# One channel group of a convolution moved to GpSimd, and the projection order of two blocks rewritten

## The chip, the cores and the metric

The kernel is written by hand for one NeuronCore of a Trainium2 chip, all in float32. The metric is the time of one execution on the device in microseconds (us), as the median of several runs. The engines are named as in the profile: PE (TensorE, matmuls), DVE (VectorE), ACT (ScalarE), POOL (GpSimd), SP (the queue that issues most transfers). Each runs its own instruction list in order; they meet only at semaphores.

## What is computed

Two stages of a transformer over 256 tokens of width 1024: two blocks of a first kind (the change touches only these), then two of a second kind. Cut to what matters, one block of the first kind is

```python
h = rms_norm(x, attn_norm_g[layer])
proj = einsum('bsd,de->bse', h, w_in[layer])
q, k_c, v_c, k_s, v_s, k_w, v_w, g_logit, u = split(proj)
q = rope_partial(rms_norm(q), positions)                  # 8 heads of 64
k_cmp, v_cmp = compress_blocks(k_c), compress_blocks(v_c) # 15 blocks of 32 tokens, a GELU MLP
k_cmp, k_slc, k_win = each rope_partial(rms_norm(k))      # 2 heads each
gates = sigmoid(g_logit)
attn_out = nsa_attention(q, k_cmp, v_cmp, k_slc, v_s, k_win, v_w, gates)
a, g = split(u, 2); y = conv(a * sigmoid(g), conv_w, 31 taps, per channel) + conv_b
conv_out = silu(layer_norm(y, ln_g, ln_b))                # 512 channels
x = x + concat(attn_out, conv_out) @ w_out[layer]
x = x + feed_forward(rms_norm(x))                         # dense in block 0, 8 experts in block 1
```

## The kernel before

The weights stream once from memory through a ring of six slots of 1 MB, in the order in which PE uses them. PE makes every product; most of the time of the kernel is PE streaming weight tiles.

The front of a block of the first kind is ordered by a table, `FRONT` (L48), which the programs of SP, PE, ACT and DVE all walk. An item is one weight tile or one small step: `u0` to `u3` (inputs of the convolution), `kv` (keys and values to be compressed), `q0`, `q1` (query heads, 4 each), `s0`, `s1` (the keys and values of two branches), `cmp0`, `cmp1` (the first products of the compression), `g` (gates), `ht`, `w2`, `gt` (small transposes and the second product of the compression), and `ada` (a tile of a matrix that only the second stage needs; 24 a block, of which 12 stand in the front to fill it).

Each item's product goes to one of two PSUM banks, `pt0` and `pt1`, strictly in turn: `bank()` (L807) counts items and takes bank n % 2, and PE waits until whoever read that bank two items earlier has emptied it. The reader is ACT for `ada` (`mod_rows`, L1577) and DVE for the others. ACT first squares the tiles of `q` and `s` (L1751, L1753) for the norm of the heads.

DVE's list, `taps(count)` (L2470), holds the convolution: a tap is one multiply-add of 128x256 for each of the 4 channel groups, all on DVE, `y` and `padded` both in SBUF:

```python
go(ve.scalar_tensor_tensor(out=y[:, cc, :], in0=src, scalar=wk, in1=y[:, cc, :],
                           op0=ALU.mult, op1=ALU.add))
```

`TAPS_AFTER` (L2538) says how many taps follow which item; 24 of the 31 stand in the front, the other 7 in `conv_beside` (L2602), 2 after each of the first attention batches. All 12 heads (8 of queries, 4 of keys) are normed and rotated together, after the last key tile and after `g`: `s1` brings one sum over the squares (L2559 to L2561) and ACT's square root, `g` the scaling (`head_scale`, L1892) and the rotation (`rotate`, L1896). Then PE transposes queries, keys and compressed keys (L1490 to L1506), DVE copies them, and the first scores can start (L894). POOL does almost nothing in this part.

## Time and profile before

| | us |
|---|---|
| median of 3 runs | 2905.27 |
| the three runs | 2900.3, 2905.27, 2907.2 |
| the profiled execution's own time | 2901.29 |
| its span, first to last instruction | 2899.5 |
| PE busy in it | 2730.1 |
| DVE busy in it | 1274.2 |
| ACT busy in it | 437.5 |
| POOL busy in it | 85.2 |

The table is read from the page of one profiled execution. Busy means that an instruction of the engine was running; an engine can be busy and yet not hold up the end. The front of the first block lies between about 30 and 146 us, that of the second between about 540 and 644 us; the attention that follows them takes some 80 us each.

### The profile page before, as it was taken

How to read it: one execution, taken by the hardware profiler on the slowest of the kernel's cores; microseconds unless marked ns; L12 is line 12 of the kernel's file. 1: busy time of each engine (PE TensorE's matmuls, PEld its weight loads, DVE VectorE, ACT ScalarE, POOL GpSimd, SP SyncE). 2: the span in 40 equal slices, each digit the busy share in tenths (PEclk: the TensorE clock that was granted, in tenths of full speed). 3: DMA queues.
4: the chain of work that ended last, by engine and by line, in shares of the span. 5: the costliest groups of instructions: out<-in, count | busy, mean ns of one | idle time of the engine just before them, and what ended most of it. 6: DMA issues, size and time to landing. Idle time of an engine off the chain costs nothing.

```text
span 2899.5 us, 49343 instructions
## 1 busy us (share of the span) xinstructions
PE 2730.1 (94%) x20757; PEld 1729.9 (60%) x20757; DVE 1274.2 (44%) x3076; ACT 437.5 (15%) x1031; POOL 85.2 (3%) x118
## 2 busy tenths in 40 slices
PE   7889999888899999999999998899989999988998
PEld 5657994665433333333333366679658967765993
DVE  1863666386301111111111155556665665233666
ACT  1131000124010110111101111400040001022100
POOL 1000000000000000000000010100000000032000
PEclk9969999988999999999999999999999999999999
DMA  8644555564499999999999955245514553122442
GB/s 260 204 146 146 164 172 174 176 203 146 168 347 397 381 409 388 385 411 387 401 398 385 403 192 105 49 145 162 174 58 145 162 174 122 67 73 61 158 167 96
DMA packets 311235, 634.95 MB, mean 219 GB/s; under 512 B 15161, under 2 KB 197825, under 8 KB 294512
## 3 DMA queue, kind: packets, MB, share of 16 engines
q1 hardware_dynamic: 305552, 616.09, 58.9%
q0 software_dynamic: 4800, 13.56, 2.6%
q8 instruction: 166, 2.72, 0.4%
q10 hardware_dynamic: 672, 2.21, 0.2%
q14 instruction: 45, 0.37, 0.0%
HBM read 623.98 MB, written 7.84 MB: 218 GB/s over the span
## 4 chain that ended last, share of the span: by engine, by line
PE 86%; DVE 9%; issue 2%; DMA 1%; POOL 1%; ACT 1%; PEld 0%; PEldq 0%; DVEq 0%; POOLq 0%; SPq 0%; ACTq 0%
PE pacc L1043 13%; PE pacc L1117 10%; PE pt L869 9%; PE pt L1117 7%; PE pt L1043 6%; PE pacc L1081 6%; PE pacc L1143 5%; PE pt L1143 5%; PE pacc L984 4%; PE po L1117 3%; PE pt L1081 3%; PE pt L1470 2%; PE pt L1022 2%; DVE bigc L2480 2%; PE pacc L894 1%
## 5 line engine op out<-in xcount | busy, mean ns | idle before, releaser
L2230 DVE TENSOR_TENSOR gateb<-kT,pt 128x512 f32<-128x512 f32 (+1 forms) x32 | 19.9, 621 | 477.6 <-PE pt L1117 476.9
L1117 PE MATMUL pacc<-ring,bigc 128*32 128x512 f32 (+1 forms) x1920 | 188.6, 550 | 4.5 <-issue 3.1
L869 PE MATMUL pt<-ring,hT 128*128 128x256 f32 x832 | 187.2, 384 | 3.6 <-issue 2.1
L869 PEld LDWEIGHTS pt<-ring,hT 128*128 128x128 f32 x832 | 157.3, 191 | 30.6 <-issue 9.3
L1043 PE MATMUL pacc<-probT,prob 128*128 128x128 f32 x1440 | 170.6, 275 | 0.0
L1043 PEld LDWEIGHTS pacc<-probT,prob 128*128 128x128 f32 x1440 | 165.6, 192 | 0.0
L1117 PEld LDWEIGHTS pacc<-ring,bigc 128*32 128x32 f32 x1920 | 68.4, 110 | 123.0 <-issue 121.0
L1117 PE MATMUL pt<-ring,bigc 128*32 128x512 f32 (+1 forms) x1280 | 139.5, 550 | 0.0
L1143 PE MATMUL pacc<-ring,bigc 128*32 128x512 f32 x864 | 137.9, 595 | 0.0
L1081 PE MATMUL pacc<-prob,chunks 128*128 128x512 f32 x282 | 136.4, 592 | 0.0
L2047 DVE TENSOR_TENSOR prob<-ring 128x512 f32<-128x512 f32 x86 | 59.5, 692 | 153.1 <-PE pacc L1043 106.4
L1143 PE MATMUL pt<-ring,bigc 128*32 128x512 f32 x1056 | 125.0, 592 | 0.0
L1625 ACT ACTIVATE prob<-prob,den 128x256 f32<-128x256 f32 (+3 forms) x192 | 99.2, 518 | 150.0 <-DVEq L1961 146.1
L984 PE MATMUL pacc<-ring,hT 128*128 128x512 f32 x256 | 111.3, 593 | 0.9 <-DVEq L2033 0.9
L842 PE MATMUL pt<-const,prob 128*128 128x128 f32 (+2 forms) x456 | 72.0, 300 | 37.0 <-DVEq L1821 33.0
L869 PE MATMUL pt<-ring,prob 128*128 128x256 f32 x448 | 103.8, 393 | 2.7 <-DVEq L2185 1.7
L2480 DVE SCALAR_TENSOR_TENSOR bigc<-big,convw,bigc 128x256 f32<-128x256 f32 x240 | 100.4, 481 | 4.4 <-DVE hid L2528 0.5
L869 PEld LDWEIGHTS pt<-ring,prob 128*128 128x128 f32 x448 | 87.9, 198 | 16.8 <-issue 3.1
L1698 ACT ACTIVATE kT<-pacc 128x512 f32<-128x512 f32 (+1 forms) x48 | 26.1, 544 | 471.2 <-PE pacc L1117 471.2
L1081 PEld LDWEIGHTS pacc<-prob,chunks 128*128 128x128 f32 x282 | 53.6, 190 | 67.4 <-issue 67.4
L1117 PEld LDWEIGHTS pt<-ring,bigc 128*32 128x32 f32 x1280 | 46.2, 110 | 77.4 <-issue 77.4
L1043 PE MATMUL pacc<-hT,ring 128*128 128x128 f32 x736 | 89.7, 275 | 0.0
(424 smaller groups left out, 4328.3 us busy)
## 6 DMA issues: line engine op xcount, KB each, us to landing
ring<-in_moe_w_down SPq DMA_DIRECT2D x80, 1024.0 KB, 13.8
ring<-in_w_gate_up SPq DMA_DIRECT2D x66, 1024.0 KB, 5.1
ring<-in_w_ada SPq DMA_DIRECT2D x48, 1024.0 KB, 5.5
ring<-in_moe_w_gate SPq DMA_DIRECT2D x48, 1024.0 KB, 6.1
ring<-in_moe_w_up SPq DMA_DIRECT2D x48, 1024.0 KB, 16.3
ring<-in_w_down SPq DMA_DIRECT2D x33, 1024.0 KB, 4.9
ring<-in_moe_w_gate SPq DMA_DIRECT2D x32, 768.0 KB, 11.4
ring<-in_moe_w_up SPq DMA_DIRECT2D x32, 768.0 KB, 8.4
```

The costliest lines, as they stand in the source:

```text
L842: return pe.transpose(dst, src, ident[0:n, 0:n])
L869: ins = pe.matmul(t[:, q * 256:q * 256 + n], src[:, k, q * P:q * P + P], w[:, k, 0:n], start=(k == 0), stop=(k == KC - 1))
L984: ins = pe.matmul(pacc[:, o:o + 512], src[:, kc, q * P:q * P + P], w[:, k, h * 512:h * 512 + 512], start=(kc == 0), stop=(kc == KC - 1))
L1022: ins = pe.matmul(pt[cc][:, j * S + lo:j * S + lo + P], tiles[j][:, k, cc * P:cc * P + P], half(k, q), start=(k == 0), stop=(k == KC - 1))
L1043: ins = pe.matmul(bank_[:, o:o + P], left(k), right(k), start=(k == 0), stop=(k == 3))
L1081: ins = pe.matmul(down_bank[m][:, 0:512], left[m], right[m], start=(g == 0), stop=(g == groups - 1), skip_group_check=True)
L1117: ins = pe.matmul(((X, Y, Z) if kind == "g" else up_bank)[r][32 * j:32 * j + 32, 0:w], hcurv[:, kc, 32 * g:32 * g + 32], moe_view(tile_)[: ...
L1143: ins = pe.matmul(banks[0 if j < 3 else i][32 * j:32 * j + 32, :], actT[:, f, 32 * g:32 * g + 32], w[:, f - 4 * t, :], start=(t == 0 and ( ...
L1470: ins = pe.matmul(t[:, h * S + lo:h * S + hi], w[:, k, h * P:h * P + P], hTv[:, k, lo:hi], start=(k == 0), stop=(k == KC - 1))
L1625: act.activation(prob[:, o:o + b.nk], prob[:, o:o + b.nk], ACT.Exp, scale=-1.0, bias=den[:, 8 + (i % 4) * 4 + j:9 + (i % 4) * 4 + j], accu ...
L2047: go(ve.tensor_tensor(s1, a21, a22, ALU.add))
L2480: go(ve.scalar_tensor_tensor(out=y[:, cc, :], in0=src, scalar=wk, in1=y[:, cc, :], op0=ALU.mult, op1=ALU.add))
```

## The change

It does four things in the two blocks of the first kind.

1. The order `FRONT`: an `ada` tile moves between `cmp0` and `s0`, and `g` moves from behind `w2` to a place ahead of `ht` and `s1`.
2. The 8 query heads are summed after `q1` and scaled and rotated after `s0`; the 4 key heads are summed after `s1` and scaled and rotated after `w2`. `qk_ready` is told twice. The square root is taken twice.
3. The fourth channel group of the convolution goes to POOL: for each tap a product into a free part of `ug` and a sum onto `y`, 31 taps a block, with semaphores. DVE's tap has three multiply-adds, and DVE waits for POOL's last tap after attention batch 3.
4. The number of taps after each item changes; their sum in the front stays 24.

```diff
-FRONT = ("ada ada cols u0 ada u1 ada u2 ada u3 ada kv ada ada q0 ada q1 ada cmp0 s0 cmp1 ada ht s1 w2 g ada gt".split(),
-         "u0 ada u1 ada u2 ada u3 ada kv ada ada q0 ada ada q1 ada cmp0 s0 ada cmp1 ada ht s1 w2 g ada gt".split())
+FRONT = ("ada ada cols u0 ada u1 ada u2 ada u3 ada kv ada ada q0 ada q1 ada cmp0 ada s0 cmp1 g ht s1 w2 ada gt".split(),
+         "u0 ada u1 ada u2 ada u3 ada kv ada ada q0 ada ada q1 ada cmp0 ada s0 cmp1 ada g ht s1 w2 ada gt".split())
...
+            for l in range(2):
+                pool.wait_ge(conv_padded, l + 1)
+                for k in range(TAPS):
+                    wk = convv[:, POOL_CHANNEL, l * TAPS + k:l * TAPS + k + 1]
+                    src = padded[:, POOL_CHANNEL, k:k + S]
+                    if k == 0:
+                        o = COL["conv_b"] + CC * l + POOL_CHANNEL
+                        pool.tensor_scalar(y[:, POOL_CHANNEL, :], src, wk, colA[:, o:o + 1], ALU.mult, ALU.add)\
+                            .then_inc(conv_tap, 1)
+                    else:
+                        pool.tensor_scalar(ug[:, k % 2, :], src, wk, None, ALU.mult).then_inc(conv_product, 1)
+                        pool.wait_ge(conv_product, l * (TAPS - 1) + k)
+                        pool.wait_ge(conv_tap, l * TAPS + k)
+                        pool.tensor_tensor(y[:, POOL_CHANNEL, :], y[:, POOL_CHANNEL, :], ug[:, k % 2, :], ALU.add)\
+                            .then_inc(conv_tap, 1)
...
+                pe.wait_ge(qk_ready, due("qk_ready"))
                 t, filled, uses, emptied = bank()
                 pe.wait_ge(emptied, uses)
                 for br in range(2):
...
-                        if item == "s1":
-                            root(small[:, 64:88])
+                        if item in ("q1", "s1"):
+                            root(head_sums[:, :, 0:8] if item == "q1" else head_sums[:, :, 8:12])
...
-                        for cc in range(CC):
+                        for cc in [c for c in range(CC) if c != POOL_CHANNEL]:
...
-                TAPS_AFTER = {"kv": 4, "q0": 5, "q1": 5, "cmp0": 3, "s0": 4, "ht": 3}
+                TAPS_AFTER = {"kv": 4, "q0": 5, "q1": 5, "cmp0": 4, "g": 1, "ht": 5}
+
+                def sum_heads(lo, hi):
+                    r = head_sums[:, :, lo:hi]
+                    link(ve.tensor_reduce(r, sqv[:, :, lo:hi, :], AX.X, ALU.add))
+                    link(ve.tensor_scalar(r, r, 1.0 / HD, EPS, ALU.mult, ALU.add))
+                    link(ve.reciprocal(r, r))
+                    tell(root_in)
+
+                def norm_heads(lo, hi):
+                    n = hi - lo
+                    ve.wait_ge(root_out, due("root_out"))
+                    heads = qkz[:, :, lo:hi, :]
+                    link(ve.tensor_tensor(heads, heads, free(head_sums[:, 0:1, lo:lo + 1], [[12, QT], [1, n], [0, HD]]),
+                                          ALU.mult))
+                    for q in range(QT):
+                        rotate(...)
+                    ve.sem_inc(qk_ready, 1)
...
                         link(ve.tensor_tensor(padded[:, :, TAPS - 1:], ug[:, 0:4, :], ug[:, 4:8, :], ALU.mult))
+                        ve.sem_inc(conv_padded, 1)
...
+                    elif item == "q1":
+                        sum_heads(0, 8)
+                    elif item == "s0":
+                        norm_heads(0, 8)
                     elif item == "s1":
...
+                        sum_heads(8, 12)
                     elif item == "w2":
+                        norm_heads(8, 12)
...
                         if i == 3:
+                            ve.wait_ge(conv_tap, (l + 1) * TAPS)
                             ve.sem_inc(conv_ready, 1)
```

The table of items says little by itself, so here is what it does to the instruction lists. The lines of the changed kernel are other numbers: its L890 is the tile product of L869, its L1433 the compression product of L1412, its L846 the `ada` product of L825.

PE, first block, from `cmp0` on, before (`bigc` in the input marks the compression, `cond` the `ada` tile, `hT` the key tile `s0`):

```order
L1412 MATMUL pt<-ring,bigc 30x128 [waits bank_emptied0,tile_loaded5,blocks_ready]
L1412 MATMUL pt<-ring,bigc 30x128 x15
L869 MATMUL pt<-ring,hT 128x256 [waits bank_emptied1,tile_loaded0]
L869 MATMUL pt<-ring,hT 128x256 x15
L1412 MATMUL pt<-ring,bigc 30x128 [waits bank_emptied0,tile_loaded1]
L1412 MATMUL pt<-ring,bigc 30x128 x15
L825 MATMUL pt<-ring,cond 32x256 [waits bank_emptied1,tile_loaded2]
L825 MATMUL pt<-ring,cond 32x256 x7
L836 MATMUL pada<-const,modrow 128x2 [waits mod_row]
```

and now:

```order
L1433 MATMUL pt<-ring,bigc 30x128 [waits bank_emptied0,tile_loaded5,blocks_ready]
L1433 MATMUL pt<-ring,bigc 30x128 x15
L846 MATMUL pt<-ring,cond 32x256 [waits bank_emptied1,tile_loaded0]
L846 MATMUL pt<-ring,cond 32x256 x7
L857 MATMUL pada<-const,modrow 128x2 [waits mod_row]
L890 MATMUL pt<-ring,hT 128x256 [waits bank_emptied0,tile_loaded1]
L890 MATMUL pt<-ring,hT 128x256 x15
L1433 MATMUL pt<-ring,bigc 30x128 [waits bank_emptied1,tile_loaded2]
L1433 MATMUL pt<-ring,bigc 30x128 x15
L1478 MATMUL pt<-hT,ring 24x256 [waits bank_emptied0,tile_loaded3]
```

The `ada` tile stands between `cmp0` and `s0`. Banks go in turn, so `s0`, which waited for bank 1, now waits for bank 0, the one that `cmp0` filled one `ada` earlier; `g` (L1478) follows `cmp1` at once.

ACT, first block, from the square of the last key tile on, before (`small` 128x24 is the root for the 12 heads, `small` 15x2 that of the compressed keys, `modrow` the copy that empties an `ada` tile's bank):

```order
L1753 ACTIVATE work<-pt 128x2x128 [waits qk_filled]
L1573 ACT_TABLE_LOAD
L1573 ACTIVATE small<-small 128x24 [waits root_in]
L1573 ACTIVATE small<-small 15x2 [waits root_in]
L1585 ACTIVATE modrow<-pt 128x256 [waits mod_filled]
```

and now, from the table load of the root of the queries on (`small` 128x2x8):

```order
L1595 ACT_TABLE_LOAD
L1595 ACTIVATE small<-small 128x2x8 [waits root_in]
L1607 ACTIVATE modrow<-pt 128x256 [waits mod_filled]
L1607 ACTIVATE modrow<-pt 128x256 [waits mod_row,mod_filled]
L1775 ACTIVATE work<-pt 128x2x128 [waits mod_row,qk_filled]
L1783 ACT_TABLE_LOAD
L1783 ACTIVATE hid<-hid 128x60 [waits hidden_raw]
L1775 ACTIVATE work<-pt 128x2x128 [waits qk_filled]
L1595 ACT_TABLE_LOAD
L1595 ACTIVATE small<-small 128x2x4 [waits root_in]
L1595 ACTIVATE small<-small 15x2 [waits root_in]
L1607 ACTIVATE modrow<-pt 128x256 [waits mod_filled]
```

The root of the queries, which comes right behind the square of `q1`, stands ahead of the copy of an `ada` tile; at the end the two roots still stand ahead of the copy of the last `ada` tile.

POOL, first block, from its last load of the start on to the second tap (before, nothing stood here behind the load `posi`):

```order
L747 DMA posi<-in_positions 15x1
L757 ISA
L757 TENSOR_SCALAR bigc<-big,convw,colA 128x256 [waits conv_padded]
L760 TENSOR_SCALAR big<-big,convw 128x256
L763 TENSOR_TENSOR bigc<-bigc,big 128x256 [waits conv_tap,conv_product]
```

Each sum waits for the product just ahead of it and for the sum of the tap before.

## Rows read from the trace of the kernel before

**Rows 1.** The page: busy by engine; chain that ended last; the group of a tap.

```profile
PE 2730.1 (94%) x20757; PEld 1729.9 (60%) x20757; DVE 1274.2 (44%) x3076; ACT 437.5 (15%) x1031; POOL 85.2 (3%) x118
...
PE 86%; DVE 9%; issue 2%; DMA 1%; POOL 1%; ACT 1%; PEld 0%; PEldq 0%; DVEq 0%; POOLq 0%; SPq 0%; ACTq 0%
...
L2480 DVE SCALAR_TENSOR_TENSOR bigc<-big,convw,bigc 128x256 f32<-128x256 f32 x240 | 100.4, 481 | 4.4 <-DVE hid L2528 0.5
```

**Rows 2.** PE timeline, first block: start us, us, what; in brackets idle before.

```profile
102.83 7.15 PE L869 MATMUL pt<-ring,hT 128*128 128x256 f32 x32 [0.26 <-issue]
...
121.08 0.41 PE L842 MATMUL pt<-const,prob 30*128 30x30 f32 x2 [5.13 <-DVEq L1821]
121.43 8.60 PE L869 MATMUL pt<-ring,hT 128*128 128x256 f32 x32
...
131.52 3.61 PE L1457 MATMUL pt<-hT,ring 128*24 128x256 f32 x16 [0.62 <-DVEq L1821]
...
140.71 1.33 PE L842 MATMUL pt<-const,big 128*128 128x128 f32 x8 [3.29 <-DVEq L2573]
143.49 1.11 PE L842 MATMUL pt<-const,big 128*128 128x128 f32 x4 [1.45 <-DVEq L1821]
...
145.87 1.04 PE L894 MATMUL pacc<-kcT,qT 64*128 64x15 f32 x8 [1.06 <-DVEq L2600]
```

**Rows 3.** PE, second block, 596 to 645 us, by line and shape: busy | idle before.

```profile
L1412 PE MATMUL pt<-ring,bigc 128*30 128x128 f32 x64 | 7.3, 273 | 1.5 <-DVEq L1821 1.5
...
L1457 PE MATMUL pt<-hT,ring 128*24 128x256 f32 x16 | 3.6, 379 | 0.6 <-DVEq L1821 0.6
L842 PE MATMUL pt<-const,big 128*128 128x128 f32 x12 | 3.1, 430 | 4.1 <-DVEq L2573 3.3 <-DVEq L1821 0.8
...
L894 PE MATMUL pacc<-kcT,qT 64*128 64x15 f32 x8 | 1.0, 376 | 1.1 <-DVEq L2600 1.1
...
L842 PE MATMUL pt<-const,prob 30*128 30x30 f32 x2 | 0.3, 231 | 1.6 <-DVEq L1821 1.6
```

**Rows 4.** Window behind the wait; last three columns: granted clock, DMA share, GB/s.

```profile
121.00:130.00 9.00, 8.92 (x34) 7.33 (x34) 5.24 (x13) 0.25 (x1) 0.00 (x0) 0.81 0.08 27
```

**Rows 5.** Timeline of DVE, first block.

```profile
80.12 1.22 DVE L2546 TENSOR_TENSOR big<-big 128x1024 f32<-128x1024 f32 x1
...
82.80 5.09 DVE L2480 SCALAR_TENSOR_TENSOR bigc<-big,convw,bigc 128x256 f32<-128x256 f32 x12
88.54 0.69 DVE L2511 TENSOR_TENSOR big<-pt,gain 128x512 f32<-128x512 f32 x1 [0.65 <-ACT work L1751]
...
131.46 1.75 DVE L2559 TENSOR_REDUCE small<-work 128x24 f32<-128x1536 f32 x1
...
136.31 1.76 DVE L1894 TENSOR_TENSOR big<-big,small 128x1536 f32<-128x1536 f32 x1 [0.26 <-DVE prob L2530]
```

**Rows 6.** Timeline of ACT, first block, end of the front.

```profile
135.59 0.20 ACT L1573 ACTIVATE small<-small 15x2 f32<-15x2 f32 x1 [1.48 <-DVEq L1821]
136.52 0.38 ACT L1585 ACTIVATE modrow<-pt 128x256 f32<-128x256 f32 x1 [0.73 <-PE pt L825]
```

**Rows 7.** One line of the program, L1969: count, duration ns min/median/max, shapes.

```profile
L1969 DVE TENSOR_TENSOR den<-den x16: 161/164/1876, 1810.9 to 2157.6; 128x4 f32<-128x4 f32 x16
```

**Rows 8.** Timeline of POOL: a sum of two inputs, and a multiply by a number.

```profile
1713.07 3.08 POOL L765 TENSOR_SCALAR biasb<-biasb 16x889 f32<-16x889 f32 x1 [3.32 <-DMA biasb<-in_na_rpb]
...
1843.30 2.36 POOL L776 TENSOR_TENSOR biasb<-biasb,const 128x1024 f32<-128x1024 f32 x1 [1.79 <-DMA biasb<-skew_scratch]
```

**Rows 9.** Timeline of DVE in the same stretch as the POOL sum.

```profile
1843.81 1.88 DVE L1969 TENSOR_TENSOR den<-den 128x4 f32<-128x4 f32 x1 [0.24 <-DVE probT L1989]
```

**Rows 10.** One line of the program, L2348.

```profile
L2348 DVE SCALAR_TENSOR_TENSOR x<-big,logit,x x4: 1283/1284/1827, 1712.5 to 1717.2; 128x1024 f32<-128x1024 f32 x4
```

**Rows 11.** Timeline of PE beside the first attention batches, first block.

```profile
166.99 0.66 PE L935 MATMUL po<-probT,big 128*64 128x128 f32 x8 [0.95 <-DVEq L2023]
...
174.48 1.22 PE L928 MATMUL po<-const 128*128 128x256 f32 x2 [1.35 <-DVEq L2023]
```

More of the change, by code:

```diff
@@ L35 @@
 TAPS = 31
+POOL_CHANNEL = 3
 CW = 512
@@ L271, in build @@
         hidden_raw = sem("hidden_raw")
+        conv_padded = sem("conv_padded")
+        conv_product = sem("conv_product")
+        conv_tap = sem("conv_tap")
         hidden_rows = sem("hidden_rows")
@@ L500, in build @@
         sqv = work[:, 0:QT * 12 * HD].rearrange("p (t h d) -> p t h d", t=QT, h=12)
+        head_sums = small[:, 64:88].rearrange("p (t h) -> p t h", t=QT)
         val1 = big[:, 1536:2048].rearrange("p (t n) -> p t n", t=QT)
@@ L512, in build @@
         turned_in = prob[0:32, 0:2 * P]
+        turned_gates = prob[0:32, 2 * P:4 * P]
         glog = small[:, 0:QT * 24].rearrange("p (t n) -> p t n", t=QT)
@@ L1436, in _ @@
                         for part in range(2):
-                            ins = transpose(t[:, part * n:part * n + n], turned_in[0:n, part * P:part * P + P], n)
+                            ins = transpose(t[:, part * n:part * n + n], (turned_in if item == "ht" else turned_gates)[0:n, part * P:part * P + P], n)
                         ins.then_inc(filled, 1)
@@ L2529, in take_front @@
                     elif item == "g":
-                        go(ve.tensor_copy(turned_in[0:24, :], t[0:24, 0:S]))
+                        go(ve.tensor_copy(turned_gates[0:24, :], t[0:24, 0:S]))
                     else:
@@ L2537, in _, with take_queries @@
                 kz = kcm[0:NCMP, 0:128].rearrange("p (h d) -> p h d", d=HD)
-                TAPS_AFTER = {"kv": 4, "q0": 5, "q1": 5, "cmp0": 3, "s0": 4, "ht": 3}
+                TAPS_AFTER = {"kv": 4, "q0": 5, "q1": 5, "cmp0": 4, "g": 1, "ht": 5}
[12 more added lines that the diff above has]
+                    for q in range(QT):
+                        rotate(qkz[:, q, lo:hi, 0:8], qkz[:, q, lo:hi, 8:16], free(cos1[:, 8 * q:8 * q + 1], [[0, n], [1, 8]]),
+                               free(sin1[:, 8 * q:8 * q + 1], [[0, n], [1, 8]]), (n, 8))
+                    ve.sem_inc(qk_ready, 1)
+                def take_queries(q):
+                    t, filled, uses, emptied = bank()
+                    ve.wait_ge(filled, uses)
+                    go(ve.tensor_copy(qTv[:, 0:4, q * P:q * P + P], t[:, :].rearrange("p (c t) -> p c t", c=4)))
+                    tell(emptied)
                 for item in FRONT[l][lead:]:
@@ L2556, in _ @@
                         tell(hidden_raw)
+                    elif item == "q1":
+                        sum_heads(0, 8)
+                    elif item == "s0":
+                        norm_heads(0, 8)
                     elif item == "s1":
-                        r = small[:, 64:88]
-                        link(ve.tensor_reduce(r, sq, AX.X, ALU.add))
-                        link(ve.tensor_scalar(r, r, 1.0 / HD, EPS, ALU.mult, ALU.add))
-                        link(ve.reciprocal(r, r))
-                        tell(root_in)
+                        sum_heads(8, 12)
                     elif item == "w2":
+                        norm_heads(8, 12)
                         head_norm(kz, 2, None, 96, work[0:NCMP, 1792:1920].rearrange("p (h d) -> p h d", d=HD))
@@ L2567, in _ @@
                         tell(gate_rows_in)
-                        ve.wait_ge(root_out, due("root_out"))
-                        head_scale(z, 24, 64)
-                        for q in range(QT):
-                            rotate(qkz[:, q, :, 0:8], qkz[:, q, :, 8:16], free(cos1[:, 8 * q:8 * q + 1], [[0, 12], [1, 8]]),
-                                   free(sin1[:, 8 * q:8 * q + 1], [[0, 12], [1, 8]]), (12, 8))
-                        ve.sem_inc(qk_ready, 1)
-                        def take_queries(q):
-                            t, filled, uses, emptied = bank()
-                            ve.wait_ge(filled, uses)
-                            go(ve.tensor_copy(qTv[:, 0:4, q * P:q * P + P], t[:, :].rearrange("p (c t) -> p c t", c=4)))
-                            tell(emptied)
                     elif item == "gt":
```

## The prediction

> **What bounds the kernel now.** I read the page first: PE is busy for 2730 of 2899.5 us and makes 86% of the chain that ended last [rows 1]. So a change pays only where PE waits. Then I read the timeline of PE through the front of the first block. From the last key tiles to the first scores it waits 5.13 us for DVE (the hidden rows of the compression, queued behind taps), 0.62, 3.29 (the norm and rotation of the heads), 1.45 and 1.06 us, in all 11.55 us [rows 2]. The reader should also compare two tile products of the same shape: 7.15 us at 102.83, but 8.60 us right behind the long wait [rows 2], where the granted clock had a mean of 0.81, a mix of its two levels, 2.4 and 1.2 GHz [rows 4]. The wait of 5.13 us thus costs another 1.45 us. In the second block the same places sum to 1.5 + 0.6 + 4.1 + 1.1 + 1.6 = 8.9 us, without a slow tile [rows 3]. Some 20 us is all that the reordering can win, under 1% of the time.
>
> DVE's own timeline says what it does meanwhile: taps, without a pause. Twelve multiply-adds take 5.09 us, so 0.42 us each; a tap of four takes 1.70 us, one of three 1.28 us [rows 5].
>
> **The order and the norm, as if POOL cost DVE nothing.** I walk through the first block. DVE has the padded input at 81.4 us (80.12 + 1.22). Four taps of 1.28 end at 86.5; the square of `q0` comes at 88.5 as before [rows 5], so DVE waits 2 us. Copy 0.8, five taps 6.4: 95.8. The square of `q1` comes about 97.6 (one tile and one `ada` later), again 1.9 us of waiting. Copy 0.8, then the sum for 8 heads, two thirds of the 1.75 us for 12 [rows 5], plus 0.5: 100.1. Five taps: 106.6, and the copy of `cmp0`: 107.0. PE is through with `cmp0` and the moved `ada` at 104.5. The moved `ada` flips the banks: `s0` now needs the bank of `cmp0` and starts at 107.0. A new wait of 2.6 us, where `s0` had none. From there the front is PE's again: `s0` 114.2, `cmp1` and `g` (3.7 and 3.61) 122.1, transposition, `s1` 129.8, `w2`. DVE's norm of the queries lies beside `cmp1` and `g`, and the hidden rows are ready in time: the waits of 5.13 and 0.62 go, and the slow tile with them. The last `ada` then waits 1.0 us until DVE has emptied the bank of `s1`.
>
> The end of the front does not gain what the edit seems to give. The 8 query heads are ready early, but their transposition needs the bank of the last `ada`, and ACT empties that bank only behind the root of the compressed keys, which stands ahead in its list. That root waits for DVE: after `s1` the sum of 4 heads (0.6 + 0.5), then their norm (a third of the 1.76 us multiply, and rotations whose cost is mostly per instruction: 12 heads took 4.4 us from 136.31 to 140.71, I take 2.6), then the compressed keys, 1.5 us as before [rows 5, 6]. From 131.6 that is 136.8, with root and copy (0.20 and 0.38) [rows 6] 137.5. PE is ready at 133.5 and waits 4.0 us where it waited 3.29 [rows 2]. Key transposition and scores wait about 2.5 us as before. Sum of PE's waits: 2.6 + 1.0 + 4.0 + 2.5 = 10.1 us. First block: 10.1 − 11.55 − 1.45 = −2.9 us. Second block, where the same list is walked: 10.1 − 8.9 = +1.2 us. `g` done earlier, a second root and table load, and the second `qk_ready` lie in waits that exist anyway: nothing. One `ada` fewer behind `s1` moves work, and adds none.
>
> Beside the attention 7 taps each lose one multiply-add, 2.9 us of DVE. PE waits there for DVE at 166.99 and 174.48, 0.95 and 1.35 us [rows 11], and a few times more; I take 2 us a block. Without any price for POOL: −2.9 + 1.2 − 4 = −5.7 us.
>
> **What POOL's taps cost DVE.** This decides. L1969 is a DVE operation of 128x4 on two SBUF inputs: 16 times, median 164 ns, once 1876 ns [rows 7]. That once it started at 1843.81 and ended at 1845.69 [rows 9]; a POOL sum of 128x1024 ran from 1843.30 to 1845.66 [rows 8]. A DVE instruction with two SBUF inputs stood still until POOL's was over. The multiply-add of L2348, also with two SBUF inputs, took 1.28 us three times and 1.83 us once [rows 10], in the time of POOL's multiply [rows 8]: a loss of 0.54 us. A tap on DVE is just such an instruction, and in the front DVE does hardly anything else.
>
> How long is a hold? The sum of 1024 columns held 2.36 us; for 256 columns 0.59 us by length, more if part of it is fixed. I take 0.65, with 0.6 to 0.8 as ends. The product by a number (889 columns) held 0.54 us; by length 0.16 us, at most the whole 0.54. I take 0.30. So 0.95 us a tap, 29 us a block. Between two holds DVE gets in: I assume turn by turn, with two to three multiply-adds for each POOL tap (POOL's own wait between product and sum leaves room), so 1.06 us of DVE work for 0.95 us of hold. Up to the copy of `cmp0` DVE has 14 taps, 17.9 us: 16 us of holds fall into them. Of these 3.9 are absorbed by the waits for `q0` and `q1` and about 1 by copies from PSUM and the reduction, which I count as free. The copy comes 11 us late, near 118 us, and PE has no other work: it waits at `cmp0` and `s0`. Later holds hide, since DVE then waits for tiles; POOL is through at 130 to 135 us, before the scores and long before batch 3, so the new wait for `conv_tap` costs nothing, nor do row multiplications of the attention.
>
> Per block +11.0. First block: 10.1 + 11.0 − 11.55 = +9.6 (the slow tile stays, behind a longer wait); second: 10.1 + 11.0 + 1.45 − 8.9 = +13.6 with a new slow tile; attention −4. **Sum +19 us** (or 22 us of delay less 2.8). The profiled execution took 2901.3 us in all (span 2899.5); the median of the runs is 4 us above it, and I forecast against the median: 2905.3 + 19 = **2924 us**.
>
> With the short holds (0.16 + 0.6) the delay is 7.3 and 5.6 us instead of 11 each, sum +10: 2915. With the long ones (0.54 + 0.8) about 22 a block, sum +41: 2946.
>
> On the length of the product's hold the Trainium skill speaks (SBUF — State Buffer, "Who interferes with whom"): whichever of the two instructions starts first keeps the shared port pair for its whole length. By that the product would hold for all its time, and not for a part. The row says 0.54 us of loss beside an instruction of 3.08 us [rows 8, 10], so I go by the row; the row of the sum agrees with the rule.
>
> For the sum the skill has a time of its own (GPSIMD Engine Reference, "3.1 Elementwise — side-by-side cycle accounting"): 4497 ns for 2048 columns. With this trace's 1024 columns that makes about 0.75 us for 256, an estimate, and the forecast would be some 6 us higher.
>
> **The rivals.**
>
> No blocking that matters: the row of 1876 ns is an exception of that instruction, or holds of 256 columns are too short to hurt. Then the −5.7 us stand: 2900 us, not slower. It decides where the hold of a tap falls under about 0.35 us, since the waits for `q0` and `q1` then swallow it. Against it: both operations that met POOL with two SBUF inputs lost time. For it: those are only two instances. Chance 0.22.
>
> DVE keeps the port through a tap: its multiply-adds overlap in time (a mean of 481 ns each, and twelve in 5.09 us) [rows 1, 5], and POOL might get in only where DVE pauses, once a tap. Then 14 holds of 0.48 us, less the absorbed 3.9, delay `cmp0` by 3 us, and POOL's leftover runs into the attention for some 3 us: 6.5 us a block, −5.7 + 13 = +7: 2912. Chance 0.15.
>
> The whole-length rule holds for the product as well, with up to 0.89 us (3.08 by length) [rows 8]: about 28 us a block, 2 x 28 − 2.8 = +53: 2958. Chance 0.05. The rule of the Trainium skill's page SBUF — State Buffer, named above, would give this case.
>
> The change does more than I count: no blocking, and ACT's copy of the last `ada` is not late, so the 4.0 us go in both blocks: 2892. Against it stand ACT's list and its root that waited for DVE before, 1.48 us [rows 6]. Chance 0.08.
>
> **How the numbers follow.** A measurement of this kernel tells 0.3%, 8.7 us, from no change. The forecast, holds turn by turn, has 0.50; nearly all of it is slower by more than that. Slower: 0.50 from the forecast, 0.04 from whole-length holds, 0.06 from DVE keeping the port, together 0.60. Same: 0.18 of no blocking and 0.10 of DVE keeping the port, 0.28. Faster: 0.08 and what is left of no blocking, 0.12. The range goes from 2898, just under the case without blocking, to 2946, the long holds; outside stay the cases of 2892 and 2958 and some of the edges.
>
> **What the new profile would show.** Right: DVE's multiply-adds of a tap have a mean well over 481 ns, with many near 1 us; PE waits 6 us or more ahead of the `s0` tile of each block; a wait near 4 us before the query transposition, ended by ACT's copy; POOL's last tap near 130 us in the first block. No blocking: multiply-adds still 0.48 us, `s0` at about 107 us. DVE keeping the port: POOL's last tap after 150 us. I am wrong if the s0 wait is there but small, or if PE's waits grow at a place that I did not name.

## The result and the profile after

Measured side by side, the kernel before has a median of 2901.65 us (20 runs, 2896.31 to 2907.73) and the changed one 2906.36 us (20 runs; one disturbed run, 9878.29 us, takes no part in the ratio, nor do two such runs of the experiments in theirs). The ratio is **1.0017, 95% interval [1.001, 1.0024]**: slower by 4.9 us, well inside the 0.3% that I had called no change. I had forecast 2924, +19 us, with slower by more than 0.3% as the likeliest case (0.60); what came, no change within 0.3%, had 0.28. The sign was right, the size was not. Of the 17.6 us between 2924 and 2906.36, 3.6 are the kernel before, which I took at 2905.3 from three runs; the other 14 are the change. The profiled execution took 2914.11 us (span 2912.3), the longest of the other 19, and what that means comes with the second profile below.

The line numbers of the profile after are 21 (PE) or 22 (DVE, ACT) higher than before's around this code. The page after, against [rows 1]:

```profile
PE 2739.0 (94%) x20757; PEld 1735.6 (60%) x20757; DVE 1281.8 (44%) x3046; ACT 440.3 (15%) x1035; POOL 194.5 (7%) x240
...
PE 86%; DVE 8%; issue 2%; DMA 1%; POOL 1%; ACT 1%; PEld 0%; PEldq 0%; DVEq 0%; POOLq 0%; SPq 0%; ACTq 0%
...
L2502 DVE SCALAR_TENSOR_TENSOR bigc<-big,convw,bigc 128x256 f32<-128x256 f32 x180 | 101.4, 616 | 4.6 <-DVE prob L2552 0.5
```

The third line is half of the answer: 60 multiply-adds are gone from DVE, and their group still takes 101.4 us, where 240 took 100.4 [rows 1]. POOL works 109 us more, and DVE is as busy as before. The timeline of PE through the first block, against [rows 2]:

```profile
99.03 3.65 PE L1433 MATMUL pt<-ring,bigc 128*30 128x128 f32 x32 [0.68 <-DVEq L1843]
...
110.66 8.54 PE L890 MATMUL pt<-ring,hT 128*128 128x256 f32 x32 [5.91 <-DVEq L1843]
...
127.25 0.28 PE L863 MATMUL pt<-const,prob 30*128 30x30 f32 x2 [0.26 <-issue]
...
140.81 1.93 PE L846 MATMUL pt<-ring,cond 128*32 128x256 f32 x16 [5.16 <-DVEq L1843]
...
146.92 1.94 PE L863 MATMUL pt<-const,big 128*128 128x128 f32 x8 [2.70 <-ACTq L1610]
149.15 1.09 PE L863 MATMUL pt<-const,big 128*128 128x128 f32 x4 [0.29 <-DVEq L1843]
...
151.51 1.04 PE L915 MATMUL pacc<-kcT,qT 64*128 64x15 f32 x8 [1.06 <-DVEq L2636]
```

The 5.13 us ahead of the hidden rows are gone. In their place stand 5.91 us ahead of `s0`, and 5.16 us ahead of the last `ada`, a wait that I had put at 1.0. The waits of over 0.4 us from `cmp0` on sum to 15.5 us (11.55 before). The same timeline in the second block, against [rows 3] (8.8 us there, 14.1 now):

```profile
615.98 10.16 PE L890 MATMUL pt<-ring,hT 128*128 128x256 f32 x32 [5.67 <-DVEq L1843]
...
648.00 1.07 PE L846 MATMUL pt<-ring,cond 128*32 128x256 f32 x16 [2.87 <-DVEq L1843]
...
654.10 1.94 PE L863 MATMUL pt<-const,big 128*128 128x128 f32 x8 [3.72 <-ACTq L1610]
```

DVE's timeline in the first block, against [rows 5], shows what PE waits for:

```profile
82.23 5.98 DVE L2502 SCALAR_TENSOR_TENSOR bigc<-big,convw,bigc 128x256 f32<-128x256 f32 x9
...
89.08 9.02 DVE L2502 SCALAR_TENSOR_TENSOR bigc<-big,convw,bigc 128x256 f32<-128x256 f32 x15
...
100.89 9.25 DVE L2502 SCALAR_TENSOR_TENSOR bigc<-big,convw,bigc 128x256 f32<-128x256 f32 x15 [0.18 <-DVE small L2566]
110.18 0.28 DVE L2548 COPY prob<-pt 30x128 f32<-30x128 f32 x1
...
130.06 9.77 DVE L2502 SCALAR_TENSOR_TENSOR bigc<-big,convw,bigc 128x256 f32<-128x256 f32 x15 [0.26 <-DVE hid L2550]
139.85 0.42 DVE L2535 TENSOR_TENSOR big<-pt,gain 128x256 f32<-128x256 f32 x1
```

Five taps of three groups take 9.02 to 9.77 us, 1.8 to 1.95 us a tap. Alone they would take 1.28 us, and a tap of four took 1.70 us. The copy of `cmp0` comes at 110.18, and `s0` starts right behind it; the bank of `s1` is taken at 139.85, behind the five taps after `ht`. POOL's timeline:

```profile
81.57 0.94 POOL L760 TENSOR_SCALAR big<-big,convw 128x256 f32<-128x256 f32 x1
82.59 0.72 POOL L763 TENSOR_TENSOR bigc<-bigc,big 128x256 f32<-128x256 f32 x1
83.30 1.08 POOL L760 TENSOR_SCALAR big<-big,convw 128x256 f32<-128x256 f32 x1
...
138.30 0.85 POOL L763 TENSOR_TENSOR bigc<-bigc,big 128x256 f32<-128x256 f32 x1
```

From the first sum to the thirtieth that is (138.30 − 82.59) / 29 = 1.92 us for each POOL tap, product and sum one behind the other; the last ends at 139.15.

### The profile page after: what moved, and what is told of

It is laid out like the page before. It is cut to its first block, busy times and chain, and to the rows that moved or that the text cites. A ratio compares the mean times of both kernels' runs of the same rounds, so it can differ in the third digit from the quotient of the medians.

```text
span 2912.3 us, 49507 instructions
## 1 busy us (share of the span) xinstructions
PE 2739.0 (94%) x20757; PEld 1735.6 (60%) x20757; DVE 1281.8 (44%) x3046; ACT 440.3 (15%) x1035; POOL 194.5 (7%) x240
## 3 DMA queue, kind: packets, MB, share of 16 engines
q8 instruction: 166, 2.72, 0.4%
## 4 chain that ended last, share of the span: by engine, by line
PE 86%; DVE 8%; issue 2%; DMA 1%; POOL 1%; ACT 1%; PEld 0%; PEldq 0%; DVEq 0%; POOLq 0%; SPq 0%; ACTq 0%
PE pacc L1064 13%; PE pacc L1138 10%; PE pt L890 9%; PE pt L1138 7%; PE pt L1064 6%; PE pacc L1102 5%; PE pacc L1164 5%; PE pt L1164 5%; PE pacc L1005 4%; PE po L1138 3%; PE pt L1102 3%; PE pt L1491 2%; PE pt L1043 2%; DVE bigc L2502 2%; PE pacc L915 2%
## 5 line engine op out<-in xcount | busy, mean ns | idle before, releaser
L890 PE MATMUL pt<-ring,hT 128*128 128x256 f32 x832 | 190.1, 388 | 15.0 <-DVEq L1843 12.8
L890 PEld LDWEIGHTS pt<-ring,hT 128*128 128x128 f32 x832 | 159.2, 194 | 42.7 <-issue 20.4
L890 PE MATMUL pt<-ring,prob 128*128 128x256 f32 x448 | 103.9, 393 | 2.7 <-DVEq L2207 1.7
L2502 DVE SCALAR_TENSOR_TENSOR bigc<-big,convw,bigc 128x256 f32<-128x256 f32 x180 | 101.4, 616 | 4.6 <-DVE prob L2552 0.5
L890 PEld LDWEIGHTS pt<-ring,prob 128*128 128x128 f32 x448 | 87.8, 197 | 16.9 <-issue 3.1
L809 POOL DMA_DIRECT2D biasb<-skew_scratch x64 | 39.0, 624 | 765.0 <-DVEq L1967 726.8
```

The lines of the kernel that those rows point to most:

```text
L890: ins = pe.matmul(t[:, q * 256:q * 256 + n], src[:, k, q * P:q * P + P], w[:, k, 0:n], start=(k == 0), stop=(k == KC - 1))
```

## The experiments

Three questions were open: what POOL's taps cost, and which of its two instructions; what the order is worth by itself; and whether the waits ahead of `s0` and the last `ada` come from the bank, from the taps, or from ACT's list. Every ratio stands against the kernel before, run on the same chip; a difference in us is the ratio less 1, times 2902. The ratio is not the quotient of the two medians and can lie up to 0.1% off it (e10: 0.9993 by the medians), so nothing is read from a difference of 2 or 3 us alone. Waits are PE's, of over 0.4 us, from `cmp0` to the first scores, in one profiled execution.

| kernel | ratio, 95% interval | us | waits, blocks 1 and 2 |
|---|---|---|---|
| before | 1 | 0 | 11.6, 8.8 |
| the change | 1.0017 [1.001, 1.0024] | +4.9 | 15.5, 14.1 |
| e1 order only | 1.0011 [0.9994, 1.0027] | +3.2 | 12.6, 12.6 |
| e2 POOL only | 0.9993 [0.9983, 1.0003] | −2.0 | 14.4, 10.0 |
| e4 the change again | 1.0014 [1.0004, 1.0023] | +4.1 | 15.4, 13.6 |
| e5 three groups | 0.9969 [0.9956, 0.9981] | −9.0 | 9.2, 9.2 |
| e6 products only | 0.9992 [0.9982, 1.0003] | −2.3 | 10.0, 9.5 |
| e8 fewer taps in front | 0.9988 [0.9977, 0.9999] | −3.5 | 9.9, 8.3 |
| e9 e8, ada's copy first | 0.9983 [0.9973, 0.9994] | −4.9 | 10.1, 9.2 |
| e10 ada back | 1.0002 [0.9993, 1.0012] | +0.6 | 10.0, 10.2 |
| e11 e8 without POOL | 0.998 [0.9971, 0.9989] | −5.8 | 5.7, 6.0 |
| e12 old order, fewer taps | 0.9981 [0.9971, 0.9992] | −5.5 | 6.2, 6.2 |
| e13 e11, ada's copy first | 0.9979 [0.997, 0.9987] | −6.1 | 6.5, 6.5 |

**e1_order_only** and **e2_pool_only** take the change apart.

```diff
 e1 (of the change)
-            for l in range(2):
-                pool.wait_ge(conv_padded, l + 1)
...
-                        for cc in [c for c in range(CC) if c != POOL_CHANNEL]:
+                        for cc in range(CC):
 e2 (of before)
+            for l in range(2):
+                pool.wait_ge(conv_padded, l + 1)
...
-                        for cc in range(CC):
+                        for cc in [c for c in range(CC) if c != POOL_CHANNEL]:
```

> The new order and the two-part norm, but DVE keeps all four channel groups of a tap and POOL has none. Theory A (from the trace of the change: a DVE tap of three groups beside POOL takes 1.80 to 1.95 us, hardly more than the 1.70 us of four groups, so POOL's share neither gained nor lost much, and the +5 us come from the order): time within 3 us of the change, about 2905, so 3 to 4 us above before; wait ahead of the s0 tile 4 to 5 us (5.91 in the change), wait of the last ada 3 to 4 us (5.16 in the change), a DVE multiply-add 0.48 us. Theory B (the order gains as the walk without blocking said, and POOL's holds cost it all): the order by itself is faster than before, about 2898.

> The old order and the single norm, with the fourth group of each tap on POOL. Theory A: a tap at 1.80 to 1.95 us instead of 1.70 delays the taps ahead of the compression's hidden rows by 2 to 3 us a block, the 7 taps beside the attention give back 1 to 2 us a block; in sum 0 to +4 us against before, 2902 to 2906. Theory B (holds of 0.95 us for each POOL tap, as forecast, all of them on the path to the first scores): +15 us or more, 2917. DVE's multiply-adds have a mean over 600 ns by both.

e1 took 2906.15 us (2905.05 before on that chip), by the ratio +3.2 us; e2 took 2901.80 us, by the ratio −2.0 us. Neither is told from zero. The timeline of PE in e1:

```profile
107.78 9.58 PE L875 MATMUL pt<-ring,hT 128*128 128x256 f32 x32 [5.07 <-DVEq L1828]
...
137.57 1.94 PE L831 MATMUL pt<-ring,cond 128*32 128x256 f32 x16 [3.72 <-DVEq L1828]
```

and in e2:

```profile
123.26 0.42 PE L861 MATMUL pt<-const,prob 30*128 30x30 f32 x2 [5.44 <-DVEq L1840]
...
144.05 1.97 PE L861 MATMUL pt<-const,big 128*128 128x128 f32 x8 [4.06 <-DVEq L2593]
```

Both new waits of the change are there without POOL, 5.07 and 3.72 us: they belong to the order together with the taps placed ahead of them. And POOL in the old order costs far less than the 15 us that the forecast's holds would have made. The waits add up: against before, e1 has +1.0 us in the first block and +3.8 in the second, e2 +2.9 and +1.2, the change +4.0 and +5.2. The times, +3.2 and −2.0 for +4.9, neither confirm nor exclude this, since the interval of e1 alone is 9.6 us wide.

**e4_change_again** is the changed kernel a second time.

> The changed kernel once more, unedited, for a second profile. The profiled execution of the change was 8 us above the median of its 20 runs, with a clock of 0.968 where the median run has 0.972. If the granted clock in the front and the attention of the two blocks makes that difference, this profile, if it is nearer to 2906, shows the same waits within 0.3 us and the difference in tiles at 1.2 GHz (the s0 tile of the second block 7.15 instead of 10.16 us). If it is waits that vary, they differ by some us.

It took 2908.03 us, ratio 1.0014 [1.0004, 1.0023]. Its front has the waits of the first profile within 0.11 us in the first block (5.92, 5.05, 2.69 and 1.06) and within 1.1 us in the second (5.69, 3.44, 2.70), but its first attention, from the first scores to the first output tile, took 72.89 us where the first profile's took 79.80. That stretch in the first profile (behind the length stand the busy times of PE, its weight loads, DVE, ACT and POOL; the first of the last three figures is the granted clock):

```profile
151.51:231.31 79.80, 73.08 (x552) 47.40 (x553) 50.10 (x217) 29.73 (x116) 0.00 (x0) 0.68 0.45 150
```

and of e4:

```profile
149.77:222.66 72.89, 64.43 (x552) 42.36 (x553) 50.13 (x217) 29.61 (x116) 0.00 (x0) 0.79 0.50 164
```

The same 552 matmuls keep PE busy for 73.08 us at 0.68 of full clock in one execution and for 64.43 us at 0.79 in another. Before had 0.73 and 79.44 us. The `s0` tile of the second block took 8.63 us in e4, 10.16 in the first profile; I had expected 7.15. So single spans can't be compared to within 7 us in this stage, and the 12.8 us between the two profiled spans can't be read as the change's. What repeats are the waits of the front, and these I use.

**e5_three_groups** leaves out of POOL's work all but the first tap of a block, so that DVE's three groups run nearly alone. (A kernel without that tap too, e3_three_groups, has no time.)

```diff
-                for k in range(TAPS):
+                for k in range(1):
```

> The change with POOL's taps left out but for the first of each block, so that nearly nothing stands in DVE's way. Left out: taps 1 to 30 of the fourth channel group, so the convolution of that group is incomplete. The walk of the prediction without blocking gives -5.7 us against before, with waits in the first block of 2.6 us ahead of the s0 tile, 1.0 us ahead of the last ada and 4.0 us ahead of the queries' transposition. Theory A (POOL holds DVE back by about 0.55 us for each DVE tap of the front): the same, -3 to -8 us against before, the whole front about 8 us shorter a block than in the change. Theory C (the order itself loses by the moved ada and by the taps behind ht): the waits stay above 2.6 and 1.0 us and the time is at before or above.

It took 2895.03 us, ratio 0.9969: 9.0 us under before, interval −12.8 to −5.5. PE:

```profile
104.81 8.78 PE L883 MATMUL pt<-ring,hT 128*128 128x256 f32 x32 [2.79 <-DVEq L1836]
...
131.39 1.07 PE L839 MATMUL pt<-ring,cond 128*32 128x256 f32 x16 [1.35 <-DVEq L1836]
...
137.50 1.94 PE L856 MATMUL pt<-const,big 128*128 128x128 f32 x8 [3.97 <-ACTq L1603]
```

The walk without blocking had 2.6, 1.0 and 4.0 us at these three places. It is right on these waits, and the other term is left: from e5 to the change it is 9.0 + 4.9 = 13.9 us for POOL's taps (8.4 to 19.8 by the ends of the two intervals), where the forecast had 24.7. One piece of the walk is not right: the slow tile was to go, but the `s0` tile of the first block takes 8.78 us. In the second block, behind a wait of 2.78 us, it takes 7.14.

**e6_products_only** and **e7_sums_only** split POOL's tap.

```diff
 e6
-                        pool.tensor_tensor(y[:, POOL_CHANNEL, :], y[:, POOL_CHANNEL, :], ug[:, k % 2, :], ALU.add)\
-                            .then_inc(conv_tap, 1)
+                        pool.sem_inc(conv_tap, 1)
 e7
-                        pool.tensor_scalar(ug[:, k % 2, :], src, wk, None, ALU.mult).then_inc(conv_product, 1)
-                        pool.wait_ge(conv_product, l * (TAPS - 1) + k)
-                        pool.tensor_tensor(y[:, POOL_CHANNEL, :], y[:, POOL_CHANNEL, :], ug[:, k % 2, :], ALU.add)\
+                        pool.tensor_tensor(y[:, POOL_CHANNEL, :], y[:, POOL_CHANNEL, :], src, ALU.add)\
```

> The change with POOL's sums left out: it computes the 30 products of each block and drops them, so the fourth channel group has only its first tap. Theory P (only an instruction of POOL with two SBUF inputs holds DVE back; the product by a number holds nothing): the DVE multiply-adds of a tap have a mean near 420 to 480 ns as without POOL, and a front like that without POOL's taps. Theory Q (the product holds as well, by 0.16 to 0.54 us each as the prediction bounded it): the mean is 500 ns or more as long as POOL's products run.

> The change with POOL's products left out: each of its 30 sums adds the shifted input itself, without its weight, so the fourth channel group is computed with weights of 1. POOL's instructions are then all of the kind with two SBUF inputs, about 0.75 us each, one behind the other. Theory P: DVE multiply-adds near 600 ns or more, for as long as POOL runs, and POOL through in about 31 x 0.75 to 31 x 1.2 us. If a sum holds DVE for its whole length (0.72 to 0.85 us), three multiply-adds beside two sums take about 2.8 us; if they take 1.3 us, the sums hold nothing and the products did.

Five DVE taps in e5, where POOL is idle:

```profile
86.80 6.53 DVE L2495 SCALAR_TENSOR_TENSOR bigc<-big,convw,bigc 128x256 f32<-128x256 f32 x15
```

in e6, beside products:

```profile
87.17 6.83 DVE L2500 SCALAR_TENSOR_TENSOR bigc<-big,convw,bigc 128x256 f32<-128x256 f32 x15
```

with its line L760 (durations in ns: least, median, longest):

```profile
L760 POOL TENSOR_SCALAR big<-big,convw x60: 922/1206/2012, 80.0 to 607.5; 128x256 f32<-128x256 f32 x60
```

and in e7, beside sums:

```profile
89.74 12.22 DVE L2499 SCALAR_TENSOR_TENSOR bigc<-big,convw,bigc 128x256 f32<-128x256 f32 x15
```

with POOL's timeline:

```profile
80.48 24.30 POOL L760 TENSOR_TENSOR bigc<-bigc,big 128x256 f32<-128x256 f32 x30
```

Products hold next to nothing: 0.30 us over some five products, 0.06 each. They are themselves slower beside taps: most take 1.21 us there, and 0.92 us from 112.3 to 115.3 us, where DVE stands idle:

```profile
113.44 0.92 POOL L760 TENSOR_SCALAR big<-big,convw 128x256 f32<-128x256 f32 x1 [0.20 <-POOL big L760]
```

Sums do hold. Thirty of them take 24.30 us, 0.81 each, and fifteen multiply-adds 12.22 us, 0.81 each too. Taken instruction by instruction the trace shows them strictly one to one, each of the fifteen starting 0.13 to 0.30 us behind a sum. So a sum takes (12.22 − 6.53) / 15 = 0.38 us from DVE. In the change, with both, it is (9.02 − 6.53) / (9.02 / 1.92) = 0.53 us for a POOL tap, so about 0.47 for its sum. That is Theory P, with a hold shorter than the sum's own 0.72 to 0.85 us. Were a sum to hold DVE even for the shortest that one took, 0.64 us (e7), a sum and a multiply-add would take 0.64 + 0.42 = 1.06 us together; they took 0.81. The Trainium skill (SBUF — State Buffer, "Who interferes with whom") says of VectorE's two-port modes that whoever issues first gets the shared pair for the whole instruction. I had carried that over to instructions with two SBUF inputs, and there it does not fit these durations: neither kind of POOL instruction stopped DVE for its length.

Two things on times. e7 took 5359.67 us because weights of 1 change the data, and with them the router's choice, so that a branch for crowded experts runs that the other profiles do not have; only its front is compared. e6 took 2900.96 us, ratio 0.9992 [0.9982, 1.0003], 6.7 us more than e5 with intervals that do not meet, though its waits differ by only 0.8 and 0.3 us. One `s0` tile of 9.42 us for 7.14 explains 2.3 us of it in the profile. From `q0` to the end of the attention the two blocks together differ by just 1.0 us in the two profiles, so the rest is not in the stretch where the products run. It stays open.

**e8_fewer_front** moves taps.

```diff
-                TAPS_AFTER = {"kv": 4, "q0": 5, "q1": 5, "cmp0": 4, "g": 1, "ht": 5}
+                TAPS_AFTER = {"kv": 4, "q0": 5, "q1": 2, "cmp0": 5, "g": 1, "ht": 3}
...
-                        taps(2)
+                        taps(3)
```

> The change with three taps fewer ahead of the copy of cmp0 (two behind q1 in place of five, five behind cmp0 in place of four), three behind ht in place of five, and three taps a batch beside the attention in place of two. Nothing is left out. If the copy of cmp0 and of s1 behind taps are what PE waits for at s0 and at the last ada, both waits fall from 5.9 and 5.1 us to under 1.5 us, and the first scores come 6 to 8 us earlier a block than in the change; beside the attention there are 4 more taps a block, 5 us more of DVE, of which I give back 1 to 3. Time 2896 to 2902. If instead the end of the front hangs on DVE's whole work and not on these two waits, the waits only move to the queries' transposition and the scores, and the time stays within 3 us of the change.

It took 2899.74 us, ratio 0.9988 [0.9977, 0.9999]: faster than the change, and than the kernel before by an interval that begins at 0.3 us. PE:

```profile
105.74 7.14 PE L890 MATMUL pt<-ring,hT 128*128 128x256 f32 x32 [0.29 <-DVEq L1843]
...
131.34 1.07 PE L846 MATMUL pt<-ring,cond 128*32 128x256 f32 x16 [0.62 <-DVEq L1843]
...
139.06 1.94 PE L863 MATMUL pt<-const,big 128*128 128x128 f32 x8 [5.41 <-ACTq L1610]
```

Both waits go, and the `s0` tile runs at full clock again (7.14 for 8.54 us). Part comes back at the transposition, where PE now waits 5.41 us for 2.70, as DVE's chain behind `s1` now bounds the end of the front.

**e9_ada_copy_first** is e8 with ACT's list turned round.

```diff
-                    elif item == "w2":
-                        root(small[0:NCMP, 96:98])
...
+                root(small[0:NCMP, 96:98])
                 act.wait_ge(gate_logits, due("gate_logits"))
```

> The kernel with fewer taps in the front (fewer_front), and ACT copies the last ada ahead of the root of the compressed keys, so that the queries' transposition no longer waits behind that root. If that wait (5.4 and 4.0 us in the two blocks) sits on the path by itself, as the prediction's rival of 2892 us had it, the first scores come 4 to 5 us earlier a block and the time falls by 6 to 9 us, to about 2892. If DVE is what the scores wait for (its chain from the copy of s1 through two norms, compressed keys and four copies from PSUM runs with hardly a pause from 130.4 to 143.7 us), the wait at the transposition goes to zero and comes back, all but 0.5 to 1 us, ahead of the key transposition or of the scores; time within 2 us of fewer_front.

2898.80 us, ratio 0.9983 [0.9973, 0.9994], which the interval of e8 does not exclude. PE:

```profile
136.46 1.12 PE L863 MATMUL pt<-const,big 128*128 128x128 f32 x4 [4.54 <-DVEq L1842]
139.40 1.08 PE L863 MATMUL pt<-const,big 128*128 128x128 f32 x4 [1.82 <-DVEq L1842]
```

The wait for ACT is gone, and 4.54 + 1.82 us for DVE stand in its place. Counted from the start of `q0`, the first scores of the first block come at 63.41 us for 63.33; counted from `s0`, those of the second come at 41.18 for 40.88. That is no gain in either. ACT's copy ended a wait that DVE would have ended just after.

**e10_ada_back** undoes the change of bank.

```diff
-... cmp0 ada s0 cmp1 ...
+... cmp0 s0 ada cmp1 ...
-                TAPS_AFTER = {"kv": 4, "q0": 5, "q1": 5, "cmp0": 4, "g": 1, "ht": 5}
+                TAPS_AFTER = {"kv": 4, "q0": 5, "q1": 5, "s0": 2, "g": 3, "ht": 2}
...
-                        taps(2)
+                        taps(3)
```

> The change with the moved ada back behind s0, so that s0 no longer needs the bank of cmp0, five taps behind q1 as in the change, and the later taps placed for it (two behind s0, three behind g, two behind ht; three a batch beside the attention). Nothing is left out. If the bank is the cause of the 5.9 us ahead of the s0 tile, s0 starts right behind cmp0 at about 104 us with no wait although DVE's copy of cmp0 is still at 110 us; the next tile that needs DVE (cmp1, bank of s0) then waits under 1.5 us. Front 6 to 8 us shorter a block than in the change, as with fewer taps; time 2896 to 2902. If s0 waits all the same, something else than the bank held it.

2900.00 us, ratio 1.0002 [0.9993, 1.0012]: within the 2896 to 2902 that I expected by its median, no gain over before by the ratio. PE:

```profile
103.32 7.14 PE L890 MATMUL pt<-ring,hT 128*128 128x256 f32 x32 [0.26 <-issue]
...
131.99 1.94 PE L846 MATMUL pt<-ring,cond 128*32 128x256 f32 x16 [2.27 <-DVEq L1843]
...
140.03 1.94 PE L863 MATMUL pt<-const,big 128*128 128x128 f32 x8 [4.62 <-ACTq L1610]
```

and DVE's copy of `cmp0`:

```profile
110.57 0.28 DVE L2548 COPY prob<-pt 30x128 f32<-30x128 f32 x1
```

`s0` starts at 103.32, right behind `cmp0`, with no wait for DVE, although `cmp0` is copied only at 110.57: it was the bank. But the sum of the front's waits is 10.0 and 10.2 us, no less than in e8.

**e11_fewer_no_pool** is e8 with all four groups on DVE (the edit of e1).

> fewer_front without POOL: same order and places of the taps, all four channel groups on DVE. A tap of the front takes 1.70 us instead of 1.80 to 1.95, so the front is as long or 1 to 2 us shorter a block than with POOL; beside the attention 11 taps cost 0.42 us more each, 4.6 us of DVE a block, of which 1 to 3 us are waited for. If POOL's share is worth anything, it is this: 0 to +4 us against fewer_front (2900 to 2904). If POOL's holds still cost more than that, this kernel is faster than fewer_front.

2896.34 us, ratio 0.998 [0.9971, 0.9989]. I expected 2900 to 2904. The interval overlaps that of e8, so what is shown is that POOL's share is worth nothing here, not that it costs. PE waits 5.7 and 6.0 us in the fronts where e8 waits 9.9 and 8.3, but more in the attention (11.9 and 12.2 us for 9.4 and 8.7): from `q0` to the attention's end e11 is 0.4 us ahead in the first block and 0.2 in the second. The front:

```profile
126.97 1.07 PE L831 MATMUL pt<-ring,cond 128*32 128x256 f32 x16 [0.62 <-DVEq L1828]
...
133.08 1.94 PE L848 MATMUL pt<-const,big 128*128 128x128 f32 x8 [3.98 <-ACTq L1595]
```

**e12_old_order_fewer** is the kernel before with four taps moved behind the front, and nothing else.

```diff
-                TAPS_AFTER = {"kv": 4, "q0": 5, "q1": 5, "cmp0": 3, "s0": 4, "ht": 3}
+                TAPS_AFTER = {"kv": 4, "q0": 5, "q1": 5, "cmp0": 2, "s0": 2, "ht": 2}
...
-                        taps(2)
+                        taps(3)
```

**e13_best** is e11 with the edit of e9.

> The kernel before, with its own order, norm and all four groups on DVE, and four taps fewer in the front: two behind cmp0 in place of three, two behind s0 in place of four, two behind ht in place of three, and three a batch beside the attention in place of two. If the gain of fewer_no_pool (-5.9 us) comes from the places of the taps alone, this kernel has it too: the wait of 5.13 us ahead of the hidden rows' transposition falls to 0 to 1 us in the first block, in the second 1.5 and 1.6 us go, the scores come 5 and 3 us earlier, the attention gives back 1 to 3 us a block; time 2896 to 2900. If the new order gains by itself, this kernel is 2 to 4 us slower than fewer_no_pool.

> fewer_no_pool with ACT's copy of the last ada ahead of the root of the compressed keys. By ada_copy_first, where that step brought the scores 0.9 to 2 us forward a block and 1 us of time within the spread, this is fewer_no_pool less 0 to 2 us: 2894 to 2897. If ACT's copy is on the path by itself, now that DVE is ahead by the blocking it lacks, 4 us a block go: under 2891.

e12: 2896.43 us, ratio 0.9981 [0.9971, 0.9992]; e13: 2896.84 us, ratio 0.9979 [0.997, 0.9987]. PE in e12:

```profile
113.59 0.30 PE L842 MATMUL pt<-const,prob 30*128 30x30 f32 x2
113.83 7.17 PE L869 MATMUL pt<-ring,hT 128*128 128x256 f32 x32
...
131.67 1.50 PE L842 MATMUL pt<-const,big 128*128 128x128 f32 x8 [3.28 <-DVEq L2573]
...
136.83 1.04 PE L894 MATMUL pacc<-kcT,qT 64*128 64x15 f32 x8 [1.06 <-DVEq L2600]
```

The wait of 5.13 us [rows 2] is gone, and the tile behind it takes 7.17 for 8.60 us, with neither the new order nor the divided norm. From `q0` to the end of the first attention e11, e12 and e13 take 138.4, 138.3 and 138.3 us; before took 144.7. In the second block it is the other way: 141.9, 141.9 and 142.2 us, where before took 138.9, since its attention there took 73.8 us and theirs 79.2 to 80.0. The attention pays much of the front's gain: in e12 PE waits 12.4 us in each of them, where before waited 8.5 and 7.9. Both blocks together gain 3.1 to 3.4 us in the profiles. With taps put off, then, the new order and the divided norm add nothing that the old order does not have, and all three are the best complete versions found, alike within their intervals.

## Why the prediction failed

By its own steps:

- **The walk of the order** held. 2.6, 1.0 and 4.0 us were forecast, 2.79, 1.35 and 3.97 measured in both blocks within 0.01 (e5). That the moved `ada` flips the banks and so makes `s0` wait for `cmp0` is shown by e10. The walk said −5.7 us, e5 measured −9.0, with −5.7 just inside its interval (−12.8 to −5.5). Its slow tile did not go in the first block (8.78 us).
- **"Attention −2 us a block"** can't be told in the time. In the profiles PE's waits there fell by 3.4 and 1.6 us; in the second profile of the same kernel by 1.7 in the first block, and rose by 1.1 in the second.
- **"So 0.95 us a tap": this is the step that failed.** That POOL holds DVE is right (616 ns for 481), and that the hold falls on taps too. The sizes are not. The product was taken at 0.30 us and measured 0.06, under the 0.16 that its length gave; the sum was taken at 0.65 and measured 0.38 to 0.47. Together 0.53 us. I had read the hold from one instruction that stood still beside a sum of 1024 columns [rows 7 to 9] and scaled it.
- **"Turn by turn, with 1.06 us of DVE work for 0.95 us of hold"** was right in kind and failed in both numbers: 1.92 us for a POOL tap leaves 1.39 of DVE work for 0.53 of hold. Up to the copy of `cmp0` the holds are 2.08 + 2.49 + 2.72 = 7.3 us (5.98, 9.02 and 9.25 us in the change, 3.90, 6.53 and 6.53 in e5), not 16. Of these the pauses for `q0` and `q1` absorb 1.97 + 1.71 us, which I had at 3.9. The copy is 3.9 us later than in e5, counted from the start of `q0` (110.18 − 80.05 us in the change, 104.33 − 78.06 in e5); I forecast 11.
- **"Later holds hide"** was wrong the other way. The five taps behind `ht` take 9.77 us, and the last `ada` waits 5.16 us, 3.8 more than in e5. The transposition behind it then waits 1.3 less. POOL's last tap ended at 139.15 us, not at 130 to 135.
- The sum by waits: 15.5 − 9.2 = 6.3 us in the first block and 14.1 − 9.2 = 4.9 in the second, with 3.0 us of slower `s0` tile in the second (10.16 for 7.14). That makes 14.2; with the second profile of the change it is 6.2 + 4.5 + 1.5 = 12.2, and the ratios say 13.9. I had 24.7.

Three of the sums beside the main one don't follow from the working above them. Taken as the 11 us were, with 4.9 us absorbed, the long holds give 17.9 x 1.34 / 1.06 − 4.9 = 17.7 us a block and not 22, so +33 us and 2938; whole-length holds give 21 and not 28, so 2945; and a sum of 0.75 us in place of 0.65 adds 3.4 us, not 6. The range would have ended some 8 us lower, and the measured time lies in it either way. It is a wide range, and lying in it confirms no step.

The rival of 2912 us, DVE keeping the port through a tap, came nearest: 14 holds of 0.48 us, `cmp0` 3 us late, 6.5 us a block. Its number for the holds is near what was measured (0.53), but by luck: they come from sums that stop DVE, at a product's cost of next to nothing, and not from DVE keeping the port. What it foretold of POOL, a last tap after 150 us, did not come: it ended at 139.15. I had it at 0.15. The case without blocking (0.22) was ruled out by the profile's page alone, and the case of 2892 us (0.08) by e9: ACT's copy, moved forward, won nothing.

What e5, e8 and e11 show that no step of mine asked: whether the taps have to stand where they stand. I priced the change against the placement that it came with. A good part of PE's wait in the front was for DVE working through taps that nobody yet needed: before, 5.3 of 11.6 us and 2.6 of 8.8 (e12), and in the change 5.6 of 15.5 and 5.7 of 14.1 (e8).

## What to carry to other kernels

Before moving work to GpSimd, ask what its instructions take back from VectorE: here a fourth of the taps moved away, and the other three fourths took as long as all had. Measured against the same kernel with all groups on VectorE, the move was worth −2.0 us in the old order, +1.7 in the new one and +2.3 with fewer taps in the front, none of them clear of zero. When a front waits for an engine that is busy with deferrable work, try first to defer more of it; one changed table (e12, −5.5 us) gave all that it gave together with a new order and a divided norm (e11, −5.8 us). A reordering that shifts a round robin of two buffers makes new pairs of waits: walk the parity, tile by tile.

## What the runs showed of the hardware

A GpSimd sum with two SBUF inputs and a VectorE multiply-add with two alternate strictly one to one (0.81 us each, e7), at a cost of 0.38 us to VectorE, about half of the sum's median of 0.72. A GpSimd product of the same size with one SBUF input costs VectorE 0.06 us, but takes longer than the sum itself: 0.92 us with VectorE idle, 1.21 us beside most multiply-adds, 2.01 us at the longest (e6). VectorE's reduction with one SBUF input took 1.22 us beside a sum as well as alone (e7, e5). Its TENSOR_SCALAR of 128x16, also with one input, once took 0.72 us beside a sum (e7) for 0.17 alone (e5), so that instructions with two SBUF inputs are not the only ones held. The granted clock of one stage differed between two executions of one program, 0.68 and 0.79, with nearly the same waits ahead of it; and the tile behind a wait of 2.8 us ran slow in one block (8.78 us) and not in the other (7.14 us, e5).
